# A two-layer transformer block on one core: the opening reordered, bias tables made later, and the last four weight units taken token tile by token tile

## What is computed

```
# first layer
x = x + rms_norm(mixer(rms_norm(x, mix_pre_g) @ w_in) @ w_out, mix_post_g)
x = x + rms_norm(cross(rms_norm(x, cross_pre_g) @ w_cq, mem) @ w_co, cross_post_g)      # gemm "co"
gate, up = split(rms_norm(x, ffn_pre_g) @ w_ffn_in)                                     # gemm "ff1"
x = x + rms_norm((silu(gate) * up) @ w_ffn_out, ffn_post_g)                             # gemm "fo1"
# second layer
x = x + nsa_mixer(rmsnorm(x, mix_norm_g), rel_bias_2, ...)                              # "in2c", "in2"
x = x + (silu(gate2) * up2) @ ffn_w_out_2                                               # "ff2", "fo2"
out = rmsnorm(x, final_norm_g)
```

## Time and profile before

| | |
|---|---|
| median of three runs | 2572.68 us (2569.11 to 2574.17) |
| the profiled execution, its own time | 2573.5 us |
| its span | 2571.7 us |
| PE busy | 2499.6 us, 97% of the span |
| ACT busy, DVE busy | 1222.0 us (48%), 1421.5 us (55%) |
| moved by DMA | 456.07 MB, mean 177 GB/s |
| weight units through ACT and DVE | 836 |

### The profile page before, as it was taken

The page is one execution under the profiler, slowest core; times in us unless marked ns, Lnnn a source line. Parts: engine busy times, 40 slices in busy tenths (PEclk is TensorE's granted clock), DMA queues, the critical chain, the costliest instruction groups (busy, mean ns, idle before and its releaser), DMA issues.

```text
span 2571.7 us, 32038 instructions
## 1 busy us (share of the span) xinstructions
PE 2499.6 (97%) x11995; PEld 2082.1 (81%) x11995; DVE 1421.5 (55%) x1912; ACT 1222.0 (48%) x1695; POOL 18.2 (1%) x33
## 2 busy tenths in 40 slices
PE   7999999997999999999998999999999999999997
PEld 6888887875888888878887898887788888888886
DVE  3468887664545444444445555676554544444444
ACT  4645446755544444434444455554544444443442
POOL 1000000000000000000000000000000000000000
PEclk9999999999999999999999999999999999999999
DMA  8665544453666666656665775343566666666664
GB/s 261 200 180 157 154 149 152 156 179 107 182 187 192 187 190 188 188 172 195 193 192 150 223 221 178 100 134 115 169 191 187 192 188 188 189 188 195 191 187 145
DMA packets 237740, 456.07 MB, mean 177 GB/s; under 512 B 16374, under 2 KB 24822, under 8 KB 236616
## 3 DMA queue, kind: packets, MB, share of 16 engines
q1 hardware_dynamic: 234408, 441.10, 56.8%
q0 software_dynamic: 3232, 13.61, 1.7%
HBM read 449.40 MB, written 5.24 MB: 177 GB/s over the span
## 4 chain that ended last, share of the span: by engine, by line
PE 91%; DVE 4%; ACT 2%; DMA 2%; issue 1%; DVEq 0%; POOL 0%; SPq 0%; ACTq 0%; POOLq 0%
PE g L309 23%; PE g L311 23%; PE g L310 23%; PE g L920 4%; PE g L922 4%; PE g L921 4%; PE g L1830 1%; PE g L1832 1%; PE g L1834 1%; PE m L950 1%; DVE wl L297 1%; DMA raw<-in_w_in 1%; PE m L674 1%; ACT wh L293 1%; ACT junk_x L512 1%
## 5 line engine op out<-in xcount | busy, mean ns | idle before, releaser
L297 DVE TENSOR_TENSOR wl<-raw,wh 128x1024 fp32r<-128x1024 f32 (+1 forms) x836 | 1015.4, 1220 | 970.6 <-ACT wh L293 967.9
L293 ACT ACTIVATE wh<-raw 128x1024 fp32r<-128x1024 f32 (+1 forms) x836 | 879.1, 1056 | 1127.0 <-PE g L311 932.2
L309 PE MATMUL g<-wh,act_hi 128*128 128x512 f32 x1824 | 718.5, 394 | 16.8 <-DVE act_lo L615 10.0
L311 PE MATMUL g<-wh,act_lo 128*128 128x512 f32 x1824 | 712.7, 391 | 0.0
L310 PE MATMUL g<-wl,act_hi 128*128 128x512 f32 x1824 | 712.3, 391 | 0.0
L309 PEld LDWEIGHTS g<-wh,act_hi 128*128 128x128 f32 x1824 | 343.9, 189 | 90.8 <-DVE act_lo L615 12.2
L311 PEld LDWEIGHTS g<-wh,act_lo 128*128 128x128 f32 x1824 | 343.8, 188 | 72.6
L310 PEld LDWEIGHTS g<-wl,act_hi 128*128 128x128 f32 x1824 | 344.2, 189 | 69.8
L309 PE MATMUL g<-wh,ht_hi 128*128 128x512 f32 x704 | 275.4, 391 | 3.1 <-DVE ht_lo L689 3.1
L311 PE MATMUL g<-wh,ht_lo 128*128 128x512 f32 x704 | 275.0, 391 | 0.0
L310 PE MATMUL g<-wl,ht_hi 128*128 128x512 f32 x704 | 274.9, 390 | 0.0
(11 more groups left out here) (340 smaller groups left out, 2160.1 us busy)
## 6 DMA issues: line engine op xcount, KB each, us to landing
raw<-in_w_ffn_in SPq DMA_DIRECT2D x176, 512.0 KB, 3.6
raw<-in_ffn_w_in SPq DMA_DIRECT2D x176, 512.0 KB, 3.7
raw<-in_w_in SPq DMA_DIRECT2D x112, 512.0 KB, 4.3
raw<-in_w_ffn_out SPq DMA_DIRECT2D x88, 512.0 KB, 3.8
raw<-in_ffn_w_out SPq DMA_DIRECT2D x88, 512.0 KB, 3.7
raw<-in_nsa_w_in SPq DMA_DIRECT2D x80, 512.0 KB, 4.4
raw<-in_w_out SPq DMA_DIRECT2D x32, 512.0 KB, 4.2
raw<-in_nsa_w_out SPq DMA_DIRECT2D x32, 512.0 KB, 4.6
```

Source lines behind the costliest of these rows:

```text
L293: nc.scalar.activation(wh[:, j % SLOTS, 0:n], raw[:, j % SLOTS, 0:n], ACT.Copy).then_inc(hi_done, 1)
L297: nc.vector.tensor_tensor(wl[:, j % SLOTS, 0:n], raw[:, j % SLOTS, 0:n], wh[:, j % SLOTS, 0:n].bitcast(F32), ALU.subtract).then_inc(lo_don ...
L309: nc.tensor.matmul(dst, h, whk, start=(first and k == 0), stop=False)
L311: ins = nc.tensor.matmul(dst, l, whk, start=False, stop=(last and k == 1))
```

## The change

**Opening.** The six rows of gains, the two bias tables and `oh_f` are issued by POOL instead of SP, ahead of POOL's constants. SP issues `ident`, then quarters of x and the first four weight units in turn. PE waits for `ident` and the gains alone before in1f; `bt` is made in `m[0:24, 0]` between in1f and in1q, copied by ACT at unit 2 of in1q, and waited for by PE before mx. ACT waits for all of x only at the squares of "n1". POOL waits for the sixteen units of in1f to be split (`lo_done`) instead of for x before it issues `masks` and `memx`.

**bc in two halves.** `oh_r` gets a place of its own and is loaded by POOL after `cross_post_g`. Fifteen small products for token tile 0 stand between co and ff1, fifteen for tile 1 between fo1 and in2c (`pe_bias_rows`), with ACT copying each half (`act_bias_rows`) behind the square root; PE waits for the copy before the bank 3 of the lead-in.

**Tail.** The last four units of fo2 are done for token tile 0, all four, and then for tile 1 (`pe_last_units`). The last chunk's adding, squares, sums, root and reciprocal go tile by tile, with a square root ahead that loads ACT's table. The result is scaled in eight pieces of 512 columns and stored in eight DMAs of 256 KB.

```diff
@@ -319,11 +320,11 @@
-        def sp_gemm(sp, name, col=lambda c: c * NB):
+        def sp_gemm(sp, name, col=lambda c: c * NB, done=0):
...
             def body(i, chunks, first):
-                for j in range(chunks * s["units"]):
+                for j in range(done if first else 0, chunks * s["units"]):
@@ -469,7 +470,27 @@
-        def pe_gemm(pe, name, hi=None, lo=None, turn=None, also={}):
+        def pe_last_units(pe, name, hi, lo):
+            s = gemms[name]
+            u0 = s["units"] - SLOTS
+            for t in range(T):
+                for j in range(SLOTS):
+                    slot = (s["u0"] + s["units"] * s["chunks"] - SLOTS + j) % SLOTS
+                    pe.wait_ge(lo_done, SLOTS + s["u0"] + s["units"] * s["chunks"] - SLOTS + j + 1)
+                    for k in range(2):
+                        whk, wlk = wh[:, slot, k * NB:(k + 1) * NB], wl[:, slot, k * NB:(k + 1) * NB]
+                        h, l = (b[:, 2 * (u0 + j) + k, t * P:(t + 1) * P] for b in (hi, lo))
+                        dst = g[:, 2 + t, :]
+                        nc.tensor.matmul(dst, h, whk, start=False, stop=False)
+                        nc.tensor.matmul(dst, h, wlk, start=False, stop=False)
+                        ins = nc.tensor.matmul(dst, l, whk, start=False, stop=(j == SLOTS - 1 and k == 1))
+                    if t == T - 1:
+                        ins.then_inc(unit_used, 1)
+                if t == 0:
+                    ins.then_inc(tile_used, 1)
+        def pe_gemm(pe, name, hi=None, lo=None, turn=None, also={}, skew=False):
@@ -482,8 +503,12 @@
                         also[j]()
+                    if skew and not first and j >= chunks * s["units"] - SLOTS:
+                        continue
...
             bodies(pe, s, body)
+            if skew:
+                pe_last_units(pe, name, hi, lo)
@@ -550,6 +575,9 @@
                 if j == n - 1:
+                    if name == "n1":
+                        for c in range(4):
+                            act.wait_ge(x_in[c], 16)
@@ -619,8 +647,12 @@
-        def after_add(name):
-            return lambda pe, b: pe.wait_ge(x_done, ADDED[name][1] + 2 * b + 2)
+        def after_add(name, rows=0):
+            def ready(pe, b):
+                pe.wait_ge(x_done, ADDED[name][1] + 2 * b + 2)
+                if b == 3 and rows:
+                    pe.wait_ge(bc_sb, rows)
+            return ready
@@ -809,7 +841,11 @@
-            return {4: first_abs, 5: on_f(1, ACT.Abs, src=f_all), 6: on_f(0, ACT.Exp, scale=-1.0),
+            def keep_bias():
+                act.wait_ge(bt_ready, 1)
+                nc.scalar.activation(bt[:, :], m[0:24, 0, :], ACT.Copy).then_inc(bt_sb, 1)
+            return {2: keep_bias, 4: first_abs, 5: on_f(1, ACT.Abs, src=f_all), 6: on_f(0, ACT.Exp, scale=-1.0),
@@ -1059,6 +1095,7 @@
             pe.wait_ge(hg_bulk, 4)
+            pe.wait_ge(bt_sb, 1)
@@ -2211,6 +2248,21 @@
+        BC_BANK = (1, 3)
+        def pe_bias_rows(pe, t):
+            pe.wait_ge(tables_in, 16 * 4)
+            for c in range(NC_):
+                o0 = P * t - CSTR * c - (CLEN - 1) + 256
+                ins = nc.tensor.matmul(m[:, BC_BANK[t], c * N_H:(c + 1) * N_H], oh_r[:, o0:o0 + P], tab[:, 8:24],
+                                       start=(c == 0), stop=(c == NC_ - 1), skip_group_check=True)
+            ins.then_inc(bc_ready, 1)
+        def act_bias_rows(act, t):
+            act.wait_ge(bc_ready, t + 1)
+            nc.scalar.activation(bc[:, t, :, :].rearrange("p c h -> p (c h)"), m[:, BC_BANK[t], 0:NC_ * N_H], ACT.Copy)\
+              .then_inc(bc_sb, 1)
@@ -2219,18 +2271,24 @@
         def _(sp):
-            sp.dma_start(oh_r[:, :], a["c_rising"]).then_inc(tables_in, 16)
-            sp.dma_start(tab[0:32, 0:8], a["rel_bias"]).then_inc(tables_in, 16)
-            sp.dma_start(tab[0:32, 8:24], a["rel_bias_2"]).then_inc(tables_in, 16)
-            sp.dma_start(oh_f[:, :], a["c_falling"]).then_inc(tables_in, 16)
             sp.dma_start(ident[:, :], a["c_ident"]).then_inc(ident_in, 16)
-            sp.dma_start(x[:, :, 0:NB], a["x"].rearrange("(t p) d -> p t d", p=P)[:, :, 0:NB]).then_inc(x_in[0], 16)
-            for n, k in enumerate(("mix_pre_g", "mem_norm_g", "cross_pre_g", "ffn_pre_g", "mix_norm_g_2", "ffn_norm_g_2")):
-                sp.dma_start(g_rows[16 * n:16 * n + 16, :], a[k].rearrange("(k p) -> k p", p=P)).then_inc(gains_in, 16)
-            for n in range(1, 4):
+            def x_cols(n):
...
                   .then_inc(x_in[n], 16)
-            sp_gemm(sp, "in1f", lambda c: c * NB + F_HG)
+            def in1f_unit(u):
+                sp_unit(sp, gemms["in1f"]["u0"] // SLOTS, u, gemms["in1f"]["w"][:, 2 * u:2 * u + 2, F_HG:F_HG + NB])
+            x_cols(0)
+            in1f_unit(0)
+            in1f_unit(1)
+            x_cols(1)
+            in1f_unit(2)
+            in1f_unit(3)
+            x_cols(2)
+            x_cols(3)
+            sp_gemm(sp, "in1f", lambda c: c * NB + F_HG, done=SLOTS)
@@ -2241,19 +2299,26 @@
             for t in range(T):
-                sp.wait_ge(fin_done, t + 1)
-                sp.dma_start(out.rearrange("(t p) d -> p t d", p=P)[:, t, :], x[:, t, :]).then_inc(out_done, 16)
-            sp.wait_ge(out_done, 32)
+                for c in range(4):
+                    sp.wait_ge(fin_done, 4 * t + c + 1)
+                    sp.dma_start(out.rearrange("(t p) d -> p t d", p=P)[:, t, c * NB:(c + 1) * NB], x[:, t, c * NB:(c + 1) * NB])\
+                      .then_inc(out_done, 16)
+            sp.wait_ge(out_done, 16 * 4 * T)
...
         def _(pool):
+            for n, k in enumerate(("mix_pre_g", "mem_norm_g", "cross_pre_g", "ffn_pre_g", "mix_norm_g_2", "ffn_norm_g_2")):
+                pool.dma_start(g_rows[16 * n:16 * n + 16, :], a[k].rearrange("(k p) -> k p", p=P)).then_inc(gains_in, 16)
+            pool.dma_start(tab[0:32, 0:8], a["rel_bias"]).then_inc(tables_in, 16)
+            pool.dma_start(tab[0:32, 8:24], a["rel_bias_2"]).then_inc(tables_in, 16)
+            pool.dma_start(oh_f[:, :], a["c_falling"]).then_inc(tables_in, 16)
...
                 pool.dma_start(lam4[:, n, :], bcast(a[k], DA_D)).then_inc(consts_in, 16)
-            pool.wait_ge(x_in[3], 16)
+            pool.wait_ge(lo_done, SLOTS + 16)
@@ -2268,6 +2333,7 @@
             pool.dma_start(g_b[:, :], bcast(a["cross_post_g"], D)).then_inc(gb_in, 16)
+            pool.dma_start(oh_r[:, :], a["c_rising"]).then_inc(tables_in, 16)
@@ -2283,35 +2349,28 @@
             pe.sem_inc(unit_used, SLOTS)
-            pe.wait_ge(tables_in, 16 * 4)
-            pe.wait_ge(tab_ready, 1)
-            nc.tensor.matmul(g[0:24, 0, :], tab[:, :], oh_f[:, :], start=True, stop=True).then_inc(bt_ready, 1)
-            for t in range(T):
-                for c in range(NC_):
-                    o0 = P * t - CSTR * c - (CLEN - 1) + 256
-                    ins = nc.tensor.matmul(g[:, 1, (t * NC_ + c) * N_H:(t * NC_ + c + 1) * N_H], oh_r[:, o0:o0 + P], tab[:, 8:24],
-                                           start=(t == 0 and c == 0), stop=(t == 1 and c == NC_ - 1), skip_group_check=True)
-            ins.then_inc(bt_ready, 1)
...
             pe.wait_ge(gains_ready, 1)
-            pe.wait_ge(bt_sb, 1)
-            pe.wait_ge(bc_sb, 1)
             pe_gemm(pe, "in1f", turn="n1")
+            pe.wait_ge(tables_in, 16 * 3)
+            pe.wait_ge(tab_ready, 1)
+            nc.tensor.matmul(m[0:24, 0, :], tab[:, :], oh_f[:, :], start=True, stop=True).then_inc(bt_ready, 1)
...
             pe_gemm(pe, "co", turn="cx")
+            pe_bias_rows(pe, 0)
...
             pe_gemm(pe, "fo1", ht_hi, ht_lo)
+            pe_bias_rows(pe, 1)
...
             turned_in(pe, "ff2", 2 * PAIRS)
-            pe_gemm(pe, "fo2", ht_hi, ht_lo)
+            pe_gemm(pe, "fo2", ht_hi, ht_lo, skew=True)
@@ -2320,10 +2379,6 @@
             act.sem_inc(pair_free[1], 1)
-            act.wait_ge(bt_ready, 2)
-            nc.scalar.activation(bt[:, :], g[0:24, 0, :], ACT.Copy).then_inc(bt_sb, 1)
-            for n in range(4):
-                act.wait_ge(x_in[n], 16)
@@ -2333,22 +2388,28 @@
             act_sqrt(act, "postcx", ss_y)
+            act_bias_rows(act, 0)
...
             act_sqrt(act, "postff", ss_y)
+            act_bias_rows(act, 1)
...
             act_ffn_in(act, "ff2", "nff2", "fo2")
-            act_gemm(act, "fo2", act_squares_x(act, "fo2", junk_a), done=AHEAD)
-            act_sqrt(act, "nfin", ss_y)
+            act_gemm(act, "fo2", act_squares_x(act, "fo2", junk_a), done=AHEAD, hold=True)
+            nc.scalar.activation(st[:, 250:251], rstd("nff2")[:, 0:1], ACT.Sqrt)
+            for t in range(T):
+                act.wait_ge(tile_added, t + 1)
+                nc.scalar.activation(junk_a[:, 1, t, :], x[:, t, 3 * NB:4 * NB], ACT.Square, accum_out=ss8[:, t, 3:4])\
+                  .then_inc(ss_done, 1)
+                act.wait_ge(var_done, NORM["nfin"] + t + 1)
```

(33 more changed lines are left out.)

10 lines of the change are left out of this document (5 added, 5 removed).

## The result

The changed kernel took 2560.74 us (median of five, 2555.96 to 2563.52), the kernel before 2573.9 beside it (five, 2569.11 to 2578.19): ratio 0.9948, 95% interval 0.9929 to 0.9966, 13.4 us less. Forecast were 2558.5 and a change of 14.2. The profiled execution took 2557.45, its span is 2555.7; between the two profiled spans lie 16.0 us.

A forecast was written before the change was run, and what follows sets the result against it. PE was taken to bound the kernel; opening -14.0, table +0.95, stall +4.5, bias rows 0 and tail -5.6 summed to -14.2, giving 2558.5 us from the median 2572.68, 8-in-10 range 2551 to 2566.

The forecast's parts named there:

- Gains and first unit: Opening: gains land at 10.5 us behind part of SP's loads, first weight unit at 14.2 instead of 23.17.
- Whoever is there first is served first: Opening's DMA queues: earlier loads go first, so 2 to 2.5 MB of SP's loads precede the last gain, about 6 us.
- Rival (c): Opening: queues take turns and gains land at 8.4 us, total 2556.5; chance 0.1.
- First to ninth unit: Opening's lead-in: 28.9 us as elsewhere in the trace, ninth unit at 43.1 instead of 57.15, 14.0 us saved.
- Table on the path: Between in1f and in1q: making the 24-row table there adds 0.95 us, at most 1.9.
- Stall in in1q: In in1q: weight units come late beside mem and the bias store, adding 4.5 us; bounds 1 and 10.
- a full ring: In in1q: weight ring full when the bias store starts, the stall's lower bound of 1 us.
- Bias rows: Gaps co to ff1 and fo1 to in2c: thirty records, 0.108 us each, 3.2 us hidden under 4.04, cost 0.
- Clock: After the two bias-row gaps: small matmuls don't hold the clock up, the first unit still runs at half clock.
- rival (b): At both gaps: small matmuls keep the clock up, saving 5.4 us more, total 2553; chance 0.15.
- Tail: Behind the last matmul: 7.9 us instead of 13.5, so 5.6 us saved; bounds 4.5 and 6.2.
- The price given for a table load: In the tail: if squares needed another ACT table, its load would come back, +1.3 us.

The follow-up runs named there:

- gains_ahead: Changed kernel with SP holding back its weight units and the rest of x until the six gain loads landed; gains in at 6.3 us.
- mem_early: Changed kernel with masks and mem issued after five in1f weight units are split instead of sixteen; ratio 0.9951 to the kernel before.
- dense_gap: Changed kernel with the first tile's bias rows replaced by fifteen 128x128 by 128x512 matmuls between co and ff1; ratio 0.9954 to the kernel before.
- unit_order: Changed kernel with its last four units taken unit by unit again, tile 0 first in each; last matmul's start to span's end 11.75 us, changed kernel 8.13.
- two_stores: Changed kernel storing the result in two 1 MB pieces instead of eight of 256 KB; last matmul's start to span's end 9.81 us, changed kernel 8.13.
- tail_alone: Kernel before with only the change's tail (tile order, eight scalings and stores, early square-root table), old opening; ratio 0.9983 to the kernel before.

## Why the prediction was right, point by point

- **Gains and first unit.** Forecast 10.5 and 14.2, measured 9.85 and 13.55 (other executions 9.2 to 10.1). The working had two errors that cancel: the landing takes 2.4 us by itself and not 4.3, and SP's loads hold it up for 3 to 4 us and not 2.1. So this term came out by luck. "Whoever is there first is served first" failed: gains landed ahead of loads that SP had issued earlier. The earlier trace rows don't carry it either, since at 16 to 18 us POOL's masks had been issued only 1.2 to 3.2 us before, and at 22 to 24 the one weight unit asked for had been issued at 22.23. Rival (c) had put the gains at 8.4, which failed too. The Trainium skill (DMA: Bandwidth & Descriptors, Queues, rings and completion order) says that each engine goes round between the queues that it has work for, a packet each. As rival (c) took it, the gains would hardly feel SP's loads; gains_ahead shows 3 to 4 us between with and without them, so the measurement decides against that reading here.
- **First to ninth unit.** Taken 28.9 from in2c, measured 28.3. That the gain was in the start and in the store's absence was right: 15.3 saved against 14.0.
- **Table on the path.** 0.95 forecast, 1.03 measured.
- **Stall in in1q.** 4.5 forecast, 5.6 measured (4.74 of it shown as idle, in pieces of 0.7 to 3.1), beside the store: the size was near and half of the reason wrong. The step let mem empty the ring ahead of the store and gave 1 us as the bound for a full ring. mem_early had the ring full and still 4.3 us of idle time, so that bound failed: the delays of the old opening were the store's own and had no need of mem. (The upper bound is wrong too: its own terms, 4 x 2.9 less 3, give 8.6 and not 10.) And the step that is missing is the clock: 5 of 8 executions pay 1 to 2.4 us more behind the stall.
- **Bias rows.** 0.117 us a record, forecast 0.108; 3.52 of the 4.04, cost 0 at the first gap. At the second in2c's first unit starts 7.35 us behind fo1's last matmul instead of 6.90, since the clock had fallen by 1370 and the transposes ran slow; it rose again earlier too, and in2c's ninth unit comes 35.4 us behind fo1's last matmul instead of 35.9. Nothing is lost.
- **Clock.** That small matmuls don't keep it and the first unit stays slow was right, and rival (b) is out; dense_gap shows in addition, in one execution, that dense ones do.
- **Tail.** 5.6 forecast, 5.78 measured, its parts borne out by unit_order, two_stores and tail_alone. The price given for a table load, 1.3, was wrong by its cover.
- **Sum.** -14.2 against -13.4 by the medians. In the traces the terms stand up: -8.6 for the opening, forecast -8.55, and -5.8 for the tail. As measured alone, though, the parts have 4.6 and 4.4, and beside the other runs of the kernel before the whole is nearer to 10 to 13. So the 0.8 between forecast and result is in part luck. The range had no term for the clock, which moves a single execution of either kernel by more than any term's error.

## What to carry to other kernels

A store read in skewed rows from few partitions is priced by how it is cut: here pieces of three heads stopped the weights and pieces with 16 rows of all heads didn't. Try such a cut, paced between the transfers that PE waits for, and read from the queue how many engines work on a piece and what engine time it takes per MB. Idle PE time of 1.6 to 4 us at full clock was often paid twice here, once as idle and again as half-clock matmuls behind it; dense matmuls into an unused bank took the second payment away in the gap before ff1. A stall costs more than its idle row says: compare starts. Before a few us are read from a pair of profiles, count the matmuls at half clock in each.

## What was not expected of the hardware

- The spread of one kernel's runs is the granted clock: of 23 runs of the kernel before, the nine with a mean clock of 0.992 have a mean span of 2568.4, the one at 0.988 has 2577.8 and the one at 0.995 has 2563.2. From 0.988 to 0.995 the clock alone would make 0.007 x 2570 = 18 us, the spans differ by 14.6.
- Slow stretches are 5 to 13 matmuls long and come at 4 to 8 places in an execution. Some places have one always (behind the gap before ff1: 13 of 13 without dense filling), others now and then (fo1: 7 of 13).
- The same 3 MB store takes 133 engine-us per MB in pieces of three heads and 49 in pieces with rows of all 24, and a piece of three heads alone under way has at most four packets in work at once.
- Small loads on POOL's queue land 2.4 us after their issue when SP's queue is nearly empty, and 5.4 to 6.2 when it has 4 MB under way.
